# Attention steps over seven groups instead of six, the heads' norms in pieces of a quarter slab, and the output heads normed in two halves

## The chip, the cores and the metric

The kernel runs on one core of a Trainium2 chip. The metric is the device time of one launch in microseconds; the median of three runs stands for a kernel. TensorE (PE, with PEld for its weight loads), VectorE (DVE), ScalarE (ACT) and GpSimd (POOL) each run their own program in order and meet on semaphores; SyncE (SP) issues the DMAs.

## The reference, cut to what matters

Two transformer blocks are computed on 512 rows of 1024 columns, in float32. The first has a retention, a differential attention and a merge of both; the second a dilated-window attention and a latent attention. The change lies in the first block's differential attention, and in the inverse root that all RMS norms of the kernel share.

```python
def rms_norm(x, g):
    xf = x.astype(jnp.float32)
    xf = xf * lax.rsqrt(jnp.mean(xf * xf, axis=-1, keepdims=True) + EPS)
    return xf * g.astype(jnp.float32)
...
        qd = rms_norm(q_d.reshape(B, S, DIFF_HEADS, 2, DIFF_DK), diff_q_norm_g[l])
        kd = rms_norm(k_d.reshape(B, S, DIFF_HEADS, 2, DIFF_DK), diff_k_norm_g[l])
        o_d = diff_attention(qd, kd, v_d.reshape(B, S, DIFF_HEADS, DIFF_DV), lam)
        o_d = rms_norm(o_d, diff_sub_norm_g[l].reshape(DIFF_HEADS, DIFF_DV)) * (1.0 - lam_init)
        o_d = (o_d.reshape(B, S, DIFF_V) * jax.nn.silu(gate_d.astype(jnp.float32))).astype(x.dtype)
        y_d = jnp.einsum('bse,ed->bsd', o_d, diff_w_o[l])
```

`diff_attention` is a causal softmax attention with 8 heads; each head takes the difference of two softmaxes. Queries and keys are 64 wide (two of each per head), values 128 wide.

## The kernel before

**Groups, slabs, quarters.** All weight products are cut into 36 groups of up to 512 output columns (`GROUPS`). A group has 8 slabs in most cases, one for each 128 rows of the weight. A slab is four quarters, one for each block `t` of 128 rows of the input. A quarter is one product in three matmuls (`mm3`, lines 1548 to 1550), since each float32 operand is split into a high and a low part. For each slab SP brings the weights into `raw` (two slabs a transfer), ACT makes `w_hi` (line 481), POOL makes `w_lo` by subtraction (line 809), both three slabs ahead, and PE sums eight slabs in the banks `Z[0..3]`. At a group's end ACT or DVE takes the banks out.

**Which groups.** Groups 10, 11, 12 and 13 give queries, keys, values and gate of the heads 0 to 3 of the differential attention; 14, 15, 16 and 17 give the same of the heads 4 to 7. Groups 18 and 19 give the merge gate, 20 and 21 multiply the attention's output by `diff_w_o`, 22 and 23 by `w_out`. From group 24 on it is the second block; its attention lies between groups 33 and 34 (`attention`), without weight products beside it.

**The attention as filler.** The differential attention goes head by head in 32 tiles (8 heads by 4 row blocks), as a chain over engines: scores (PE, line 1680), bias and row extreme (DVE, line 1280), exponent (ACT, line 650), scaling (POOL, line 915), combination (DVE, line 1299), transposes (PE, line 1706), split (ACT 645, DVE 1286), output product (PE). Each engine has the chain as a generator of 86 steps, and `diff_due(v)` says how many steps are to be issued by quarter `v` of the attention's groups. In the kernel before these are groups 14 to 19 (`G_DIFF0 = 14`), 192 quarters: 36 steps by quarter 83, 22 more by 129, the last 28 by 163. An engine's program holds the same step at the same quarter as the others', and PE does its quarter's product first. So a step waits for a step before it of another engine, and has as cover the quarters between both. The first queries and keys are transposed at slab 5 of group 13.

**Norms of queries and keys.** The heads of groups 10 and 11 are normed before the attention begins; those of 14 and 15 within it, in slabs 1 to 5 of the group after. In `diff_slot` POOL squares one row block a slab (line 821, behind `lo`), DVE begins the slab with the sums of these squares (`head_sums`, line 1060), and at slab 5 it does `head_scale` in one piece: the inverse root (`rsqrt`, a seed and four Newton passes of three instructions; `link` makes each wait for the one before) and four scalings of 512 columns (line 1072). The transposes of head 4 wait for them (`head_normed`).

**Norm of the output.** A head's output in `A[3]` is squared by ACT (line 661) and multiplied by the gate into `o_sb` (DVE, line 1292, `o_out`). After all eight, at slab 4 of group 19, `scale_heads(diff=True)` makes the 32 inverse roots and scales `o_sb` in four pieces of 1024 columns (line 1156, `o_normed`). The transposes of `o_sb` for group 20 (`turn_when_ready`, line 1558) begin at slab 4 of group 19 and wait for all of it.

**Other users of `rsqrt`.** The norms of the rows (`row_rms`, in groups 0 and 24, ahead of DVE's part of the fifth transposed input block), the retention's heads, the latent vectors, and queries and keys of the second block.

## Time and profile before

| | us |
|---|---|
| median of the three runs | 1064.23 |
| lowest, highest | 1055.76, 1064.32 |
| profiled execution | 1065.86 |
| its span, first to last instruction | 1064.1 |
| PE busy, share of the span | 993.1, 93% |
| DVE, ACT, POOL busy | 449.7, 446.0, 498.1 |
| mean granted TensorE clock | 0.953 |

The profiled execution lies 1.6 us above the median of the runs. The engines' busy times overlap. PE's record holds every matmul; as matmuls are pipelined, a busy PE is not a PE at its peak, but an idle PE is lost time wherever it sets the end. A time in brackets behind a row is idle time of that engine just before it, with what ended it.

### The profile page before, as it was taken

Reading aid. Unit: us, or ns where it says so; the run is one execution under the profiler, and the core shown is the slowest. Engines: PE = TensorE matmul, PEld = TensorE weight load, DVE = VectorE, ACT = ScalarE, POOL = GpSimd, SP = SyncE. Lnnn points to the kernel's source line nnn. Section 1 sums busy time; section 2 is a strip of 40 time slices with the busy share of each in tenths; the row PEclk is TensorE's granted clock in tenths of the full one; section 3 lists DMA queues with packets and bytes.
Section 4 is the critical chain, followed back from the end, with each engine's and each line's share of the span. In section 5 each row is a group of like instructions: output and inputs, shape, how many; then the busy total and the mean of one; then the engine's idle time right before and its main releaser. Section 6 shows DMA issues by size and latency. Waiting matters only on the chain.

```text
span 1064.1 us, 14047 instructions
## 1 busy us (share of the span) xinstructions
PE 993.1 (93%) x5116; PEld 809.0 (76%) x5116; DVE 449.7 (42%) x1084; ACT 446.0 (42%) x992; POOL 498.1 (47%) x476
## 2 busy tenths in 40 slices
PE   6999989999999999797999899999999979999998
PEld 5777788876888877576777687788878756778877
DVE  3300478133204333545455523326552466458811
ACT  4333552334233345354565233236335315458821
POOL 2443534434457365354454334433754554545542
PEclk9999999999999999898999999999999985569999
DMA  6332211323333231111221241222422320110023
GB/s 203 97 83 77 80 40 41 99 59 99 99 89 105 84 93 50 47 51 40 60 61 40 65 174 60 99 79 76 118 75 85 88 80 20 30 31 2 2 64 115
DMA packets 41171, 78.76 MB, mean 74 GB/s; under 512 B 3296, under 2 KB 5088, under 8 KB 41104
## 3 DMA queue, kind: packets, MB, share of 16 engines
q1 hardware_dynamic: 41104, 77.87, 24.5%
q8 instruction: 41, 0.67, 0.3%
q14 instruction: 26, 0.21, 0.1%
HBM read 75.74 MB, written 2.12 MB: 73 GB/s over the span
## 4 chain that ended last, share of the span: by engine, by line
PE 69%; DVE 12%; issue 6%; ACT 6%; POOL 5%; DMA 1%; SPq 1%; ACTq 0%; DVEq 0%; POOLq 0%
PE Z L1548 20%; PE Z L1550 19%; PE Z L1549 19%; POOL w_lo L809 3%; PE A L1548 2%; PE A L1680 1%; PE A L1770 1%; PE A L1550 1%; PE A L1549 1%; PE A L1558 1%; ACT prob L697 1%; DVE rs_b L1028 1%; DVE rstd L1029 1%; DMA raw<-in_w_in 1%; POOL prob L821 1%
## 5 line engine op out<-in xcount | busy, mean ns | idle before, releaser
L809 POOL TENSOR_TENSOR w_lo<-raw,w_hi 128x512 fp32r<-128x512 f32 (+2 forms) x262 | 340.1, 1306 | 435.5 <-ACT w_hi L481 435.2
L1548 PE MATMUL Z<-w_hi,hT_hi 128*128 128x512 f32 (+1 forms) x832 | 336.8, 405 | 14.1 <-DVE hT_lo L1044 4.6
L1550 PE MATMUL Z<-w_hi,hT_lo 128*128 128x512 f32 (+1 forms) x832 | 325.9, 392 | 0.0
L1549 PE MATMUL Z<-w_lo,hT_hi 128*128 128x512 f32 (+1 forms) x832 | 325.6, 391 | 0.0
L481 ACT CAST w_hi<-raw 128x512 fp32r<-128x512 f32 (+2 forms) x262 | 157.5, 615 | 281.4 <-PE Z L1550 267.5
L1548 PEld LDWEIGHTS Z<-w_hi,hT_hi 128*128 128x128 f32 x832 | 157.9, 190 | 55.3 <-POOL w_lo L809 6.9
L1550 PEld LDWEIGHTS Z<-w_hi,hT_lo 128*128 128x128 f32 x832 | 157.6, 189 | 33.0
L1549 PEld LDWEIGHTS Z<-w_lo,hT_hi 128*128 128x128 f32 x832 | 158.1, 190 | 27.7
L1548 PE MATMUL Z<-w_hi,oT_hi 128*128 128x512 f32 x128 | 51.6, 403 | 3.3 <-DVE tmp L1101 2.2
L945 POOL TENSOR_SCALAR prob<-prob,rinv 128x128 f32<-128x128 f32 (+1 forms) x64 | 34.0, 532 | 36.9 <-DVE rinv L1363 35.6
L1550 PE MATMUL Z<-w_hi,oT_lo 128*128 128x512 f32 x128 | 50.1, 391 | 0.0
L1549 PE MATMUL Z<-w_lo,oT_hi 128*128 128x512 f32 x128 | 49.9, 390 | 0.0
L1060 DVE TENSOR_REDUCE stat<-bias 128x8 f32<-128x512 f32 (+2 forms) x32 | 18.4, 583 | 63.2 <-POOL bias L821 63.2
L650 ACT ACTIVATE x_sb<-x_sb,nmax 128x128 f32<-128x128 f32 (+3 forms) x64 | 35.5, 557 | 20.5 <-DVE nmax L1280 20.5
L1370 DVE TENSOR_TENSOR pT_lo<-A,pT_hi 128x128 fp32r<-128x128 f32 (+1 forms) x64 | 31.0, 484 | 27.5 <-ACT pT_hi L694 26.7
L694 ACT CAST pT_hi<-A 128x128 fp32r<-128x128 f32 (+1 forms) x64 | 26.8, 419 | 34.8 <-PE A L1770 34.6
L697 ACT ACTIVATE prob<-prob,nmax 128x128 f32<-128x128 f32 (+1 forms) x64 | 36.1, 564 | 11.9 <-DVE nmax L1347 11.9
L1121 DVE TENSOR_TENSOR x_sb<-x_sb,Z 128x512 f32<-128x512 f32 x16 | 10.9, 688 | 64.6 <-PE Z L1550 64.6
L1770 PE MATMUL A<-ident,prob 128*128 128x128 f32 x160 | 36.8, 338 | 0.7 <-POOL prob L945 0.7
L1280 DVE CUSTOM_DVE_ANT_0 x_sb<-A,bias 128x128 f32<-128x128 f32 (+3 forms) x64 | 28.7, 486 | 18.1 <-PE A L1680 18.0
L495 ACT ACTIVATE z_sb<-Z,rms 128x512 f32<-128x512 f32 (+1 forms) x40 | 26.5, 680 | 19.6 <-PE Z L1550 19.6
L1044 DVE SCALAR_TENSOR_TENSOR oT_lo<-A,cols,oT_hi 128x512 fp32r<-128x512 f32 x16 | 12.0, 751 | 48.3 <-ACT oT_hi L529 48.3
(286 smaller groups left out, 1716.2 us busy)
## 6 DMA issues: line engine op xcount, KB each, us to landing
raw<-in_w_in SPq DMA_DIRECT2D x92, 512.0 KB, 3.8
raw<-in_w_out SPq DMA_DIRECT2D x16, 512.0 KB, 3.6
raw<-in_ret_w_o SPq DMA_DIRECT2D x8, 512.0 KB, 3.5
raw<-in_diff_w_o SPq DMA_DIRECT2D x8, 512.0 KB, 3.5
x_sb<-in_x SPq DMA_DIRECT2D x8, 256.0 KB, 6.2
x_sb<-in_x SPq DMA_DIRECT2D x4, 512.0 KB, 5.7
bias<-bias_dram SPq DMA_DIRECT2D x8, 256.0 KB, 3.1
out<-x_sb SPq DMA_DIRECT2D x8, 256.0 KB, 3.2
```

Of the source, the lines that this page charges most:

```text
L481: act.copy(w_hi[:, s % SPLIT_SLOTS, 0:width], raw[:, c % RAW_SLOTS, s - CHUNK_START[c], 0:width]).then_inc(hi_ready, 1)
L650: act.activation(p, p, ACT.Exp, bias=nmax[:, j, n:n + 1], scale=-1.0, accum_out=rsum[:, n, j:j + 1]).then_inc(s_exp, 1)
L694: act.copy(pT_hi[:, m % 2, 0:wm], turn_bank(ph, m)[:, 0:wm]).then_inc(p_hi, 1)
L697: act.activation(prob_at(ph, 0, n, w), prob_at(ph, 0, n, w), ACT.Exp, bias=nmax[:, 0, n % 32:n % 32 + 1], scale=-1.0, accum_out=rsum[:, n ...
L809: pool.tensor_tensor(w_lo[:, s % SPLIT_SLOTS, 0:width], raw[:, c % RAW_SLOTS, s - CHUNK_START[c], 0:width], w_hi[:, s % SPLIT_SLOTS, 0:wid ...
L945: pool.tensor_scalar(p0, p0, rinv[:, m % 32, 0:1], 0.5, ALU.mult, ALU.mult).then_inc(s_scaled, 1)
L1280: dve.tensor_tensor_reduce(prob_at(DIFF, j, n, w), A[j][:, 0:w], bias[:, h % 2, S - w:S], -1.0, TOP, ALU.add, ALU.min, nmax[:, j, n:n + 1] ...
L1370: dve.tensor_tensor(pT_lo[:, m % 2, 0:wm], turn_bank(ph, m)[:, 0:wm], pT_hi[:, m % 2, 0:wm], ALU.subtract).then_inc(p_lo, 1)
L1548: pe.matmul(out, l_hi, r_hi, start=first, stop=False)
L1549: pe.matmul(out, l_hi, r_lo, start=False, stop=False)
L1550: return pe.matmul(out, l_lo, r_hi, start=False, stop=last)
L1770: last = pe.transpose(turn_bank(ph, m)[:, kk], prob_at(ph, 0, m, S)[:, kk], ident[:, :])
```

## The change

- The groups of the attention are 13 to 19 instead of 14 to 19: 224 quarters. The steps are due from quarter 10 on, and the last at quarter 208 of these (quarter 176 counted as before). The first transposes of queries and keys move from slab 5 to slab 1 of group 13.
- POOL squares two row blocks in each of the slabs 0 and 1 of groups 15 and 16; DVE takes the sums at four places two quarters apart.
- `head_scale` is a generator of eight pieces, one in each quarter of slabs 3 and 4: three times a part of the inverse root, then part and scalings.
- `scale_heads(diff=True)` becomes `diff_heads_normed(half)`, once for heads 0 to 3 in slabs 5 and 6 of group 17, once for heads 4 to 7 in the same slabs of group 19. The first four transposes of `o_sb` wait for the first half alone, the next four for the second. The one into `A[3]` waits for the last head's output to be taken.
- `rsqrt` has three Newton passes instead of four, for all its users.

```diff
-G_QD, G_DIFF, G_DIFF0, G_DIFF1 = 10, 13, 14, 19
+G_QD, G_DIFF, G_DIFF0, G_DIFF1 = 10, 13, 13, 19
...
+DIFF_FIRST, DIFF_SECOND, DIFF_THIRD, DIFF_LAST = 10, 116, 160, 208
...
 def diff_due(v):
-    if v < 84:
-        return 36 * (v + 1) // 84
-    if v < 130:
-        return 36 + 22 * (v - 83) // 46
-    return min(86, 58 + 28 * (v - 129) // 34)
+    if v < DIFF_FIRST:
+        return 0
+    if v < DIFF_SECOND:
+        return 36 * (v - DIFF_FIRST + 1) // (DIFF_SECOND - DIFF_FIRST)
+    if v < DIFF_THIRD:
+        return 36 + 22 * (v - DIFF_SECOND + 1) // (DIFF_THIRD - DIFF_SECOND)
+    return min(86, 58 + 28 * (v - DIFF_THIRD + 1) // (DIFF_LAST - DIFF_THIRD))
...
+def normed_in(g):
+    return in_diff(g) and g - 1 in HEAD_NORM and g - 1 > G_DIFF
...
-                if g - 1 in HEAD_NORM and 1 <= k <= TT:
-                    c0, t = HEAD_NORM[g - 1], k - 1
-                    pool.wait_ge(z_by_act, act_evacs[g - 1] + t + 1)
-                    square(z_sb[:, t, c0:c0 + 512], 512, diff=True)
-                for _ in range(diff_due(v + 3) - diff_due(v - 1)):
-                    next(steps)
+                if g == G_DIFF0 and k == 1:
+                    diff_bias(0)
+                    diff_values(0)
+                for half in range(2):
+                    if normed_in(g) and k < 2:
+                        c0, t = HEAD_NORM[g - 1], 2 * k + half
+                        pool.wait_ge(z_by_act, act_evacs[g - 1] + t + 1)
+                        square(z_sb[:, t, c0:c0 + 512], 512, diff=True)
+                    for _ in range(diff_due(v + 2 * half + 1) - diff_due(v + 2 * half - 1)):
+                        next(steps)
...
-            def rsqrt(n, parts=range(5)):
+            def rsqrt(n, parts=range(4)):
...
-                rsqrt(32)
+                for part in range(4):
+                    rsqrt(32, (part,))
+                    if part < 3:
+                        yield
                 for t in range(TT):
+                    yield
                     zz = z_sb[:, t, c0:c0 + 512].rearrange("p (h e) -> p h e", h=8)
...
+            def diff_heads_normed(half):
+                n = H // 2 * (half + 1)
+                dve.wait_ge(o_squared, TT * n)
+                dve.wait_ge(o_out, n)
...
+                for t in range(TT):
+                    yield
+                    o = o_sb[:, t, 512 * half:512 * half + 512].rearrange("p (h e) -> p h e", h=H // 2)
+                    r = rstd[:, 4 * t:4 * t + 4].unsqueeze(2).broadcast_to([P, H // 2, DV])
+                    dve.tensor_tensor(o, o, r, ALU.mult).then_inc(o_normed, 1)
...
-                if g - 1 in HEAD_NORM and 1 <= k <= TT:
-                    head_sums(k - 1, squares_d)
-                if g - 1 in HEAD_NORM and k == TT + 1:
-                    head_scale(HEAD_NORM[g - 1])
                 for t in range(TT):
+                    if normed_in(g) and 2 <= TT * k + t <= 8 and t % 2 == 0:
+                        head_sums(2 * k + t // 2 - 1, squares_d)
                     for _ in range(diff_due(v + t) - diff_due(v + t - 1)):
                         next(steps)
+                    if normed_in(g) and k in (3, 4):
+                        next(norms[g])
+                    if g == G_DIFF0 + 4 and k in (5, 6):
+                        next(norms["first"])
+                    if g == G_DIFF1 and k in (5, 6):
+                        next(norms["second"])
...
-                        pe.wait_ge(o_normed, 8)
+                        pe.wait_ge(o_normed, 4 * (half + 2))
...
+                if g == G_DIFF_OUT and k == 3:
+                    pe.wait_ge(o_out, H)
...
-                    if k == START_SLAB and g == G_DIFF:
+                    if k == 1 and g == G_DIFF0:
```

## Rows read from the trace of the kernel before

**Rows 1.** The page: engines' busy time over the span, and granted clock in 40 slices.

```profile
PE 993.1 (93%) x5116; PEld 809.0 (76%) x5116; DVE 449.7 (42%) x1084; ACT 446.0 (42%) x992; POOL 498.1 (47%) x476
...
PEclk9999999999999999898999999999999985569999
```

**Rows 2.** Windows at the group borders 13 to 19: length, each engine's busy time, PEclk.

```profile
356.30:380.20 23.90, 23.28 (x106) 18.71 (x105) 2.57 (x4) 8.77 (x16) 11.95 (x10) 1.00 0.22 65
...
411.10:456.60 45.50, 38.01 (x196) 29.63 (x196) 20.91 (x63) 19.61 (x53) 20.32 (x20) 0.92 0.17 47
456.60:501.50 44.90, 36.88 (x195) 28.09 (x194) 23.23 (x70) 20.37 (x62) 20.49 (x21) 0.92 0.17 48
...
583.30:614.30 31.00, 26.92 (x126) 22.13 (x125) 15.48 (x25) 11.06 (x25) 11.49 (x8) 0.94 0.21 68
sum 258.00, PE 236.00 PEld 184.58 DVE 116.23 ACT 125.47 POOL 116.77; mean PE 33.71 PEld 26.37 DVE 16.60 ACT 17.92 POOL 16.68
```

**Rows 3.** A window over group 11, a group without attention beside it.

```profile
312.80:334.50 21.70, 21.70 (x97) 17.98 (x96) 10.63 (x23) 7.43 (x13) 14.20 (x12) 1.00 0.34 97
```

**Rows 4.** Waits of PE, 356.3 to 614.3: us in total, times, longest.

```profile
PE A L1663 <- DVE z_sb L1072: 5.6, 1, 5.6
PE A L1663 <- DVE pT_lo L1286: 5.1, 3, 3.3
PE A L1680 <- DVE nmax L1280: 4.4, 2, 2.9
PE A L1558 <- DVE o_sb L1156: 4.1, 1, 4.1
PE A L1548 <- DVE o_sb L1292: 2.2, 4, 0.9
PE Z L1548 <- POOL w_lo L809: 0.5, 1, 0.5
```

**Rows 5.** Timelines of POOL, DVE and PE in slab 3 of group 15.

```profile
427.09 1.04 POOL L821 TENSOR_TENSOR prob<-z_sb 128x512 f32<-128x512 f32 x1
...
428.16 0.69 DVE L1060 TENSOR_REDUCE stat<-prob 128x8 f32<-128x512 f32 x1 [2.69 <-POOL prob L821]
...
430.28 0.33 PE L1680 MATMUL A<-kT_hi,qT_hi 64*128 64x128 f32 x2 [2.94 <-DVE nmax L1280]
```

**Rows 6.** Timelines of DVE and POOL: `head_scale` in groups 15 and 16.

```profile
438.64 1.29 POOL L809 TENSOR_TENSOR w_lo<-raw,w_hi 128x512 fp32r<-128x512 f32 x1 [1.43 <-ACT w_hi L481]
...
438.78 1.19 DVE L1028 SCALAR_TENSOR_TENSOR rs_b<-rs_b,rs_a 128x32 f32<-128x32 f32 x1
440.01 0.19 DVE L1029 SCALAR_TENSOR_TENSOR rstd<-rs_b,rstd 128x32 f32<-128x32 f32 x1
440.24 0.19 DVE L1027 TENSOR_TENSOR rs_b<-rstd 128x32 f32<-128x32 f32 x1
...
482.36 0.18 DVE L1068 TENSOR_SCALAR rs_a<-stat 128x32 f32<-128x32 f32 x1
...
486.69 2.50 DVE L1072 TENSOR_TENSOR z_sb<-z_sb,rstd 128x512 f32<-128x512 f32 x4
```

**Rows 7.** Timeline of DVE in group 19: inverse roots and scalings of the output.

```profile
587.43 0.18 DVE L1147 TENSOR_SCALAR rs_a<-stat 128x32 f32<-128x32 f32 x1
...
592.97 6.80 DVE L1156 TENSOR_TENSOR o_sb<-o_sb,rstd 128x1024 f32<-128x1024 f32 x4
```

**Rows 8.** Windows over the four stretches of lower clock in groups 15, 16 and 19, summed.

```profile
sum 17.10, PE 14.97 PEld 12.04 DVE 4.89 ACT 5.82 POOL 4.92; mean PE 3.74 PEld 3.01 DVE 1.22 ACT 1.45 POOL 1.23
```

**Rows 9.** Timeline of DVE in group 12: the last scalings ahead of the attention.

```profile
351.83 3.60 DVE L1072 TENSOR_TENSOR z_sb<-z_sb,rstd 128x512 f32<-128x512 f32 x4
```

**Rows 10.** Timelines of PE and DVE: waits outside groups 13 to 19.

```profile
29.17 0.50 PE L1548 MATMUL Z<-w_hi,hT_hi 128*128 128x512 f32 x1 [2.25 <-DVE hT_lo L1044]
...
724.53 0.16 DVE L1029 SCALAR_TENSOR_TENSOR rstd<-rs_b,rstd 128x4 f32<-128x4 f32 x1
...
856.49 0.79 PE L1548 MATMUL Z<-hT_hi,w_hi 128*128 128x512 f32 x1 [2.93 <-POOL w_lo L809]
```

**Rows 11.** Windows of the second attention, line 1347 alone: length, DVE busy, PEclk.

```profile
885.30:929.90 44.60, 7.89 (x33) 0.50 0.09 26
967.20:1006.80 39.60, 11.73 (x49) 1.00 0.01 2
```

More of the change, by code:

```diff
@@ L713, in diff_slot @@
                 hi(s + 3)
+                if g == G_DIFF0 and k == 1:
+                    diff_queries(0)
+                    diff_keys(0)
+                    diff_values(0)
                 if g + 1 in EARLY and k >= 4:
@@ L956, in diff_slot @@
                 lo(SLAB0[g] + k + 3)
-                if g - 1 in HEAD_NORM and 1 <= k <= TT:
-                    c0, t = HEAD_NORM[g - 1], k - 1
-                    pool.wait_ge(z_by_act, act_evacs[g - 1] + t + 1)
-                    square(z_sb[:, t, c0:c0 + 512], 512, diff=True)
-                for _ in range(diff_due(v + 3) - diff_due(v - 1)):
-                    next(steps)
+                if g == G_DIFF0 and k == 1:
+                    diff_bias(0)
+                    diff_values(0)
+                for half in range(2):
[5 more added lines that the diff above has]
+                        next(steps)
             steps = diff()
@@ L984, in _ @@
                         retention(k)
-                    if k == START_SLAB + 1 and g == G_DIFF:
-                        diff_bias(0)
-                        diff_values(0)
                     if k == START_SLAB + 1 and g == G_ATT2:
@@ L1037, in query_norms @@
                 rsqrt(64, (part,))
-                if part == 4:
+                if part == 3:
                     dve.engine_nop().then_inc(latent, 1)
@@ L1078, in head_norm @@
                     head_sums(t, bias)
-                head_scale(c0)
+                for _ in head_scale(c0):
+                    pass
             def take(g, t):
@@ L1137, in take_gates, with scale_heads @@
                                                  ALU.mult).then_inc(th_used, 1)
-            def scale_heads(diff=False):
-                if diff:
-                    dve.wait_ge(o_squared, TT * H)
-                    dve.wait_ge(o_out, H)
-                else:
-                    dve.wait_ge(sq_used, count["sq"])
-                sums = stat[:, 32:64] if diff else stat[:, 0:32]
-                link(dve.tensor_scalar(rs_a[:, 0:32], sums, 1.0 / DV, EPS, ALU.mult, ALU.add))
+            def diff_heads_normed(half):
+                n = H // 2 * (half + 1)
+                dve.wait_ge(o_squared, TT * n)
+                dve.wait_ge(o_out, n)
+                sums = stat[:, 32:64].rearrange("p (t h) -> p t h", t=TT)[:, :, n - H // 2:n]
+                link(dve.tensor_scalar(rs_a[:, 0:16].rearrange("p (t h) -> p t h", t=TT), sums, 1.0 / DV, EPS,
+                                       ALU.mult, ALU.add))
+                for part in range(4):
+                    rsqrt(16, (part,))
+                    if part < 3:
+                        yield
+                r4 = rstd[:, 0:16].rearrange("p (t h) -> p t h", t=TT)
+                link(dve.tensor_tensor(r4, r4, rms[:, 0, 0, :].unsqueeze(2).broadcast_to([P, TT, H // 2]), ALU.mult))
+                for t in range(TT):
+                    yield
+                    o = o_sb[:, t, 512 * half:512 * half + 512].rearrange("p (h e) -> p h e", h=H // 2)
+                    r = rstd[:, 4 * t:4 * t + 4].unsqueeze(2).broadcast_to([P, H // 2, DV])
+                    dve.tensor_tensor(o, o, r, ALU.mult).then_inc(o_normed, 1)
+                yield
+            def scale_heads():
+                dve.wait_ge(sq_used, count["sq"])
+                link(dve.tensor_scalar(rs_a[:, 0:32], stat[:, 0:32], 1.0 / DV, EPS, ALU.mult, ALU.add))
                 rsqrt(32)
-                if diff:
-                    r4 = rstd[:, 0:32].rearrange("p (t h) -> p t h", t=TT)
-                    link(dve.tensor_tensor(r4, r4, rms[:, 0, 0, :].unsqueeze(2).broadcast_to([P, TT, H]), ALU.mult))
                 for t in range(TT):
@@ L1305, in diff, with diff_slot @@
                     yield
-            def diff_slot(g, k, steps):
+            def diff_slot(g, k, steps, norms):
                 v = TT * (KD * (g - G_DIFF0) + k)
-                if g - 1 in HEAD_NORM and 1 <= k <= TT:
-                    head_sums(k - 1, squares_d)
-                if g - 1 in HEAD_NORM and k == TT + 1:
-                    head_scale(HEAD_NORM[g - 1])
+                if g == G_DIFF0 and k == 1:
+                    diff_queries(0)
+                    diff_keys(0)
                 for t in range(TT):
+                    if normed_in(g) and 2 <= TT * k + t <= 8 and t % 2 == 0:
+                        head_sums(2 * k + t // 2 - 1, squares_d)
                     for _ in range(diff_due(v + t) - diff_due(v + t - 1)):
                         next(steps)
+                    if normed_in(g) and k in (3, 4):
[4 more added lines that the diff above has]
+                        next(norms["second"])
                     if k == KD - 1:
@@ L1474, in _ @@
             steps = diff()
+            norms = {G_DIFF0 + 2: head_scale(HEAD_NORM[G_DIFF0 + 1]), G_DIFF0 + 3: head_scale(HEAD_NORM[G_DIFF0 + 2]),
+                     "first": diff_heads_normed(0), "second": diff_heads_normed(1)}
             for g in range(NG):
@@ L1477, in _ @@
                     for k in range(KD):
-                        diff_slot(g, k, steps)
+                        diff_slot(g, k, steps, norms)
                     continue
@@ L1821, in project @@
                         pe.wait_ge(pair_lo, k + 1)
-                    if k == START_SLAB and g == G_DIFF:
+                    if k == 1 and g == G_DIFF0:
                         pe.wait_ge(head_normed, 8)
```

14 lines of the change are left out of this document (4 added, 10 removed).

## The prediction

> **What bounds the kernel now.** I read the page first. PE is busy for 93% of the span, and no other engine for half of it [rows 1]. So PE's own program sets the end, and a change can give back only three things: PE's idle time, a lower granted clock under its work, and PE's work itself. The change takes no matmul away. The question is how much of the first two lies where the change works.
>
> Windows at the group borders come next. Groups 13 to 19 take 258.0 us with 236.0 us of busy PE, so PE idles for 22.0 us there [rows 2]. A group without attention beside it takes 21.7 us with PE never idle [rows 3]. The idle time is not spread: groups 15 and 16 hold 7.5 and 8.0 us of it, group 19 holds 4.1 us, and in just these three the mean clock is below 1 [rows 2].
>
> The waits of PE in this stretch name the causes, 21.9 us in all [rows 4]. The reader should see that five of the six rows end on DVE, though DVE is busy for only 116.2 us of the 258.0 us [rows 2]. DVE is not short of time; it is late at certain places. The timelines show them. In slab 3 of group 15 POOL's square ends at 428.13, DVE's sum starts at 428.16 after 2.69 us of idleness, the row extremes of the attention queue behind it, and PE gets its scores going at 430.28, 2.94 us late [rows 5]. `head_scale` in group 16 runs from 482.36 to 489.19 [rows 6], and the transposes of head 4 wait 5.6 us for it [rows 4]. The norm of the output runs from 587.43 to 599.77 [rows 7], and the transposes of `o_sb` wait 4.1 us.
>
> Last the clock. Four stretches of together 17.10 us were granted half speed (1.2 instead of 2.4 GHz) in groups 15, 16 and 19. They hold 14.97 us of PE's work [rows 8], and each follows a wait of 2.9 us or more. Work at half speed takes twice the time, so they cost 14.97 / 2 = 7.5 us.
>
> **The change part by part.** What could be won in groups 13 to 19 is 21.9 + 7.5 = 29.4 us, and the stretch would take 228.6 us.
>
> Sums of squares. Before, every slab from 1 to 4 begins on DVE with a wait for POOL, whose square stands behind `w_lo` of the same slab. Waits of this kind are both of line 1280 (4.4 us) and two of the three on line 1286 (5.1 less the longest 3.3, 1.8 us), together 6.2 us [rows 4]. After, the squares are done in slabs 0 and 1, two each. The first sum stands at quarter 2 of slab 0. With slabs of about 4.5 us beside the attention, quarter 2 comes 2.2 us after the slab's start. The square is ready after `w_hi`, `w_lo` (1.3 us) and its own 1.04 us [rows 5, 6], and ACT still has a bank of the last group to empty: some 4 us. DVE is then late by 2 us there and by less at each next sum. The cover is what counts: in the first phase a step is due every 106/36 = 2.9 quarters of 1.1 us, 3.2 us, where it was 84/36 = 2.3 quarters, 2.6 us. And with the new order no step with row extremes of group 16 lies right behind the first sum. I take 0.5 us as what stays. From both sides: nothing, or the whole 6.2 us and as much again if POOL, with two squares a slab, makes both DVE and its own scaling late.
>
> Scaling of queries and keys. One piece of 6.8 us (482.36 to 489.19) [rows 6] becomes eight. An instruction of the inverse root comes 0.23 us after the last (440.01 to 440.24), and there are 12 of them instead of 15 with the first one: 2.8 us. A scaling takes 2.50 / 4 = 0.63 us. So a piece takes about 0.7 us and lies in a quarter of 1.1 us, in which the attention needs DVE for 0.4 us on average. It has the cover of 2.9 quarters, so it is priced at nothing. The last piece is at quarter 3 of slab 4, and the transposes of head 4's keys are at quarter 1 of slab 5. Gone: 5.6 us and the longest of line 1286 (3.3 us). Without that cover, each of the pieces would cost PE its length.
>
> A row speaks against pieces beside POOL: while `w_lo` ran at 438.64, an instruction of 0.19 us took 1.19 us [rows 6]. The Trainium skill (GPSIMD Engine Reference, section Specifications) says that the SBUF interfaces are shared with VectorE and that instructions with two SBUF inputs contend. By that rule, if each of 32 pieces were held once, DVE would spend 32 us more. The row has one instruction held in each POOL operation, in the kernel before too, and the sum goes by it.
>
> Norm of the output. The first half is done two groups early. The second half has its roots and scalings (2.8 + 4 × 0.63, about 5.4 us) in slabs 5 and 6 of group 19, while PE needs it only after slab 0 of group 20, two to three slabs of 3 us later. Gone: 4.1 us. What is late next is the last head's own output, which only the transpose into `A[3]` at slab 7 needs, over three slabs after the last step: nothing.
>
> Spread of the steps. The last 28 steps are due over 48 quarters instead of 34. The waits for line 1292 (2.2 us) are of outputs close behind one another; I leave 0.5 us. The 0.5 us of `w_lo` in group 13 stays and moves with the first transposes. The 86 steps cost PE the same work wherever they stand. The start at slab 1 of group 13 waits for scalings that end at 351.83 + 3.60 = 355.4 [rows 9], and PE reaches that slab 2.7 us after 356.3: nothing. If it were late, it would be by tenths. SP's loads of `x` behind the last step are held by the waits on `p_t` and `s_comb`; these move by 13 quarters, and the transfers are for group 22: nothing.
>
> With no wait near 3 us left, the four stretches of half speed go: 7.5 us. The Trainium skill (TensorE: Matmul & The Clock Gate, section Terms) gives the penalty as the throttled time times one less the ratio, here 17.10 / 2 = 8.6 us. The rows give 7.5 us, since PE was idle in a part of them; the difference is 1.1 us.
>
> In the stretch: 29.4, less 0.5 (sums), 0.5 (line 1292), 0.5 (`w_lo`), and 0.5 for pieces that come late once: 27.4 us.
>
> Three Newton passes. In `row_rms` three instructions less, 0.2 us apart (0.16 us busy) [rows 10], stand in front of what PE waits for in group 0 (2.25 us) and in the like place of group 24: 2 × 0.6 = 1.2 us. The 2.93 us wait for `w_lo` in group 33 [rows 10] has a square of POOL before it that waits for DVE's roots: 3 × 0.23 = 0.7 us. Elsewhere the roots lie beside work of PE. From nothing to 3 us, the upper if one of the shorter waits no longer brings a slow stretch.
>
> Sum: 27.4 + 1.9 = 29.3 us. The profiled execution of 1065.86 (span 1064.1 and 1.8 around it) becomes 1036.6. It stands 1.6 above the median of the runs, 1064.23; the forecast of the median is 1064.2 − 29.3 = 1035 us.
>
> **The rivals.**
>
> *The sums still stall PE.* For it: POOL gets 3.4 us of `w_lo` and squares into a slab of 4.5 us, and its scalings wait for DVE, which waits for its squares. Against it: the first steps of group 16 with row extremes come a slab later. The 6.2 us less 0.5 and one slow stretch (1.7 us) stay: 1035 + 7.4 = 1042 us; with twice the waits 1050 us.
>
> *The pieces stand in PE's way.* Four series of 2.8 + 2.5 = 5.3 us, all on the path, are 21 us: 1056 us. It decides once a step's cover is under a piece of 0.7 us plus its step. Against it: the dense end of the attention (0.82 steps a quarter) had idle PE for 0.9 us at most [rows 4].
>
> *The second attention runs at half speed for less time.* Line 1347 leaves two records a tile, eight a head. At clock 0.50 four heads took 44.6 us (33 records), at full clock six took 39.6 us (49 records) [rows 11]: 11.2 us a head against 6.6 us. So the clock there is worth far more than all waits. The three runs of one kernel lie 8.6 us apart, which I read as this. The shift could put it into the shorter case: 1035 − 8.6 = 1026 us. The Trainium skill (the same page, Part 1) says that the gate runs free of the kernel's start and that results vary by run; by that rule the shift favours no side, which is why this rival is small.
>
> *The other sign: it runs at half speed to its end.* Eight heads more at 4.6 us each are 37 us: 1072 us. From 29.3 / 4.6 = 6.4 heads more on, the gain is eaten. For it: the stretch begins after a wait of the gates ahead of it, which the change leaves. Against it: the runs shown lie within 8.6 us, less than two heads' worth.
>
> **How the numbers follow.** Chances: the forecast 0.55, sums still stall 0.20, shorter half speed 0.13, pieces in the way 0.07, longer half speed 0.05. The forecast's own range, from its open ends (nothing to 3 us outside, 0 to 4 us inside), is 1030 to 1041 us. The range of 8 in 10 takes in the second and third case with their spread, 1024 to 1050 us, and leaves out the last two. 1% is 10.6 us, about what a measurement can tell from no change; faster by more means below 1053.6. The first three cases lie below, 0.88; the fourth is within, with a part of the last: 0.09; slower keeps 0.03.
>
> **What would show it.** Groups 13 to 19 should take 230 to 232 us instead of 258.0. In PE's waits there, line 1072 and the output's scaling should be gone, and lines 1280 and 1286 together be under 1 us. The clock should be 1.00 in each group's window. DVE's scalings should stand singly between rows of the attention. The transposes of `o_sb` in group 19 should have no wait. It is wrong if new waits of over 1 us stand on POOL's squares or in slabs 3 and 4, or if the low slices of PEclk at the second attention (8, 5, 5, 6) [rows 1] become more or fewer.

## The result and the profile after

| | before | after |
|---|---|---|
| median, us | 1064.28 (4 runs, 1055.76 to 1065.07) | 1025.74 (4 runs, 1020.73 to 1034.31) |
| profiled execution and its span | 1065.86, 1064.1 | 1022.06, 1020.2 |
| mean granted TensorE clock | 0.953 | 0.979 |

The ratio is 0.966, with a 95% interval of 0.958 to 0.975. The ratios in this document and their intervals leave out runs that lay over 1.5% above the fastest of the same kernel; medians and ranges hold all runs. The forecast was 1035 us, range 1024 to 1050. The median moved by 38.5 us where 29.3 were forecast.

The spans of the two profiled executions differ by 43.9 us. Read at the group borders, they come from these places. Each is a difference of two windows or of two starts of a group.

| stretch | before | after | difference |
|---|---|---|---|
| start to group 13 | 356.3 | 352.2 | −4.1 |
| groups 13 to 19, the attention of the change | 258.0 | 233.5 | −24.5 |
| groups 20 to 32 | 228.7 | 227.4 | −1.3 |
| group 33, up to the second attention's first row extreme | 37.3 | 35.4 | −1.9 |
| second attention, to group 34 | 136.8 | 123.3 | −13.5 |
| groups 34 and 35 | 47.0 | 48.5 | +1.5 |

The page of the changed kernel first: the row of busy times and the granted clock in 40 slices, as in [rows 1].

```profile
PE 969.3 (95%) x5116; PEld 791.5 (78%) x5116; DVE 447.3 (44%) x1062; ACT 444.3 (44%) x992; POOL 501.2 (49%) x476
...
PEclk9999999999999999999999999999999997959999
```

PE has the same 5116 matmuls and 23.8 us less busy time, since less of its work was done at half speed. The slices below 9 in the middle are gone, and at the second attention there are fewer.

The windows over groups 13 to 19 of the changed kernel (columns as in [rows 2]), and PE's waits in them (as in [rows 4]):

```profile
352.20:378.90 26.70, 26.44 (x133) 20.65 (x131) 6.65 (x22) 13.44 (x31) 14.34 (x13) 1.00 0.27 83
...
411.00:442.20 31.20, 31.20 (x172) 24.66 (x170) 21.67 (x55) 16.74 (x44) 19.68 (x19) 1.00 0.22 68
442.20:478.10 35.90, 33.87 (x194) 26.29 (x192) 23.89 (x62) 19.18 (x55) 19.69 (x19) 1.00 0.19 60
...
556.70:585.70 29.00, 28.60 (x152) 23.59 (x151) 14.64 (x33) 13.20 (x31) 12.65 (x10) 1.00 0.22 73
sum 233.50, PE 228.85 PEld 179.31 DVE 122.01 ACT 123.82 POOL 116.95; mean PE 32.69 PEld 25.62 DVE 17.43 ACT 17.69 POOL 16.71
```

```profile
PE A L1699 <- DVE z_sb L1088: 2.0, 1, 2.0
PE A L1699 <- DVE pT_lo L1316: 1.0, 1, 1.0
PE A L1584 <- DVE o_sb L1324: 0.8, 2, 0.4
PE A L1716 <- DVE nmax L1310: 0.4, 1, 0.4
PE Z L1584 <- POOL w_lo L819: 0.3, 1, 0.3
PE Z L1584 <- DVE o_sb L1109: 0.2, 1, 0.2
```

Groups 15 and 16 went from 45.5 and 44.9 us [rows 2] to 31.2 and 35.9. The clock is 1.00 in every group in this profile. The waits fell from 21.9 us [rows 4] to 4.7. PE's busy time, 228.85 us, is what the prediction had as the stretch without any wait or slow clock (228.6 us). One wait of 2.0 us is left in group 16, again on the scaling of the keys.

The second attention, 13.5 us of the gain, holds none of the parts of the change that the forecast priced. Of the change it has only the shorter inverse roots of its queries. Windows over it and over its two stretches of half speed, in the changed kernel:

```profile
848.50:971.80 123.30, 116.29 (x916) 95.70 (x915) 91.19 (x307) 82.63 (x236) 71.40 (x105) 0.87 0.07 18
847.40:861.10 13.70, 13.42 (x50) 10.23 (x50) 10.59 (x41) 8.18 (x22) 6.93 (x10) 0.50 0.09 20
895.20:915.70 20.50, 20.50 (x105) 15.86 (x104) 10.08 (x34) 9.22 (x25) 6.99 (x12) 0.50 0.02 8
```

The same in the kernel before:

```profile
880.30:1017.10 136.80, 131.78 (x914) 107.73 (x915) 93.01 (x310) 82.74 (x236) 71.44 (x105) 0.74 0.06 17
...
879.80:937.80 58.00, 57.21 (x266) 43.74 (x266) 32.61 (x114) 26.86 (x77) 31.23 (x44) 0.50 0.08 24
944.60:958.30 13.70, 13.70 (x70) 10.60 (x68) 7.10 (x23) 6.22 (x18) 3.18 (x7) 0.50 0.02 8
```

The matmuls are the same in number; half speed lasted 71.7 us before and 34.2 us after.

### The profile page after: what moved, and what is told of

Read it like the earlier page. It is cut to its first block, busy times and chain, and to the rows that moved or that the text cites. A ratio compares the mean times of both kernels' runs of the same rounds, so it can differ in the third digit from the quotient of the medians.

```text
span 1020.2 us, 14034 instructions
## 1 busy us (share of the span) xinstructions
PE 969.3 (95%) x5116; PEld 791.5 (78%) x5116; DVE 447.3 (44%) x1062; ACT 444.3 (44%) x992; POOL 501.2 (49%) x476
## 4 chain that ended last, share of the span: by engine, by line
PE 73%; DVE 10%; ACT 6%; issue 5%; POOL 5%; DMA 1%; SPq 1%; ACTq 0%; DVEq 0%; POOLq 0%
PE Z L1584 22%; PE Z L1586 21%; PE Z L1585 21%; POOL w_lo L819 2%; PE A L1584 2%; PE A L1716 2%; PE A L1586 1%; PE A L1585 1%; PE A L1594 1%; ACT prob L707 1%; PE A L1806 1%; DMA raw<-in_w_in 1%; PE A L1742 1%; ACT w_hi L491 1%; DVE m_sb L1134 1%
## 5 line engine op out<-in xcount | busy, mean ns | idle before, releaser
L1585 PEld LDWEIGHTS Z<-w_lo,hT_hi 128*128 128x128 f32 x832 | 156.6, 188 | 27.4
L1806 PE MATMUL A<-ident,prob 128*128 128x128 f32 x160 | 32.8, 307 | 2.8 <-POOL prob L955 2.7
L655 ACT CAST pT_hi<-A 128x128 fp32r<-128x128 f32 (+3 forms) x32 | 13.7, 427 | 47.6 <-PE A L1742 47.5
```

Source lines behind the costliest of these rows:

```text
L1585: pe.matmul(out, l_hi, r_lo, start=False, stop=False)
L1806: last = pe.transpose(turn_bank(ph, m)[:, kk], prob_at(ph, 0, m, S)[:, kk], ident[:, :])
```

## The experiments

The stretch of groups 13 to 19 is named "the stretch" here. Its length in a profile is the sharp measure, since kernels that share its code agree in it by a few tenths of a microsecond plus what the clock does in it. What the clock does is not little. Two of the experiments below, "square early" and "latent steps spread", leave the stretch as the changed kernel has it, and their profiles show the same waits, to 0.1 us. Yet in both a stretch of 3.4 us at half speed came after the 2.0 us wait in group 16. Their windows over groups 13 to 19, in this order:

```profile
353.40:588.40 235.00, 230.33 (x1265) 180.11 (x1265) 121.97 (x334) 123.91 (x338) 117.16 (x113) 0.99 0.22 64
357.90:592.90 235.00, 230.35 (x1266) 180.14 (x1265) 121.96 (x334) 124.00 (x338) 116.94 (x113) 0.99 0.22 64
```

So the same code took 233.5, 235.0 and 235.0 us, and 1.5 us of a difference can be the clock alone. The median of the whole program is blurred by the clock at two places. One lies about 165 us from the start: in six of the fourteen profiles, with edits of the kernel before and of the changed one among them, 10.2 or 13.7 us at half speed lie there, and group 13 begins at 357.6 to 359.2 us instead of 352.1 to 356.3. The other is the second attention. Together they show in the unchanged kernel: the kernel before had medians of 1064.37 (7 runs), 1064.74 (13), 1054.47 (17) and 1054.15 us (11) on the four occasions on which it was run beside the experiments (each on another chip), and single runs from 1046.45 to 1072.49 us.

### Three passes alone

```diff
-            def rsqrt(n, parts=range(5)):
+            def rsqrt(n, parts=range(4)):
```

> The kernel before with three Newton passes instead of four, nothing else. Groups 13 to 19 should keep their 258 us less 1.4 (two times three instructions of 0.23 us in the pieces that stall PE). Theory 'phase' (the 15.5 us that group 33 with the second attention lost between before and after, 174.2 to 158.7, are a matter of where the clock's state falls, not of the edit): about 1064 - 2 - 1.4 = 1061 us, and half speed in the second attention for about as long as before, some 70 us. Rival 'roots' (the shorter query norms at the start of the second attention keep the clock up): 1064 - 3 - 15 = 1046 us, with half speed there for under 40 us.

Measured 1046.9 us (1039.3 to 1049.2) beside 1064.4, ratio 0.986 (0.978 to 0.995). The stretch took 255.9 us, 2.1 less than before where 1.4 were expected: 0.8 us of idle time and one stretch of half speed fewer. The second attention took 121.5 us. By the numbers on record this spoke for the rival. The next run tells otherwise.

### Four passes in the changed kernel

```diff
-            def rsqrt(n, parts=range(4)):
+            def rsqrt(n, parts=range(5)):
```

> The changed kernel with four Newton passes as before; the fifth part of each root stands with the fourth piece. Theory 'phase': 1026 + 2 = 1028 us, group 33 stays near 159 us; pieces a little longer, the wait of 2.0 us for line 1088 in group 16 grows by under 1 us. Rival 'roots': group 33 goes back to 174 us, total 1043 us.

Measured 1031.7 us (1029.4 to 1034.1). The second attention took 121.3 us with four passes. So the roots don't set its clock, and the rival falls. The stretch took 236.3 us, 2.8 more than the changed kernel's profile: 1.3 us of idle time and one stretch of 3.4 us at half speed. That stretch came with three passes too, in the two profiles shown above, and against their 235.0 us the fourth pass costs 1.3 us.

### The output's norm at once

```diff
-                    if g == G_DIFF0 + 4 and k in (5, 6):
-                        next(norms["first"])
-                    if g == G_DIFF1 and k in (5, 6):
-                        next(norms["second"])
...
                 if g + 1 in EARLY and k >= 4:
+                    if k == 4:
+                        for _ in norms["first"]:
+                            pass
+                        for _ in norms["second"]:
+                            pass
```

> The changed kernel, but the output heads' two halves are both normed at slab 4 of group 19, one behind the other. Theory 'the halves save their wait': the transposes of o_sb wait for the first half, about 5 us with 2.8 us of roots and 2.5 us of scalings, and one stretch of half speed (1.7 us) returns: +5 to +7 us on groups 13 to 19, 1032 us. Rival 'the wait is hidden anyway since the steps end where the transposes begin': +1 us or less.

The stretch took 241.5 us, 8.0 more than with the halves; the forecast was +5 to +7. The median does not show it (1025.5 us). PE's waits in the stretch of this kernel:

```profile
PE A L1595 <- DVE o_sb L1175: 5.9, 1, 5.9
PE A L1700 <- DVE z_sb L1088: 2.0, 1, 2.0
```

The wait for the output's scaling is back, and longer than the 4.1 us of before, because the attention now ends right in front of the transposes. Idle time in the stretch rose by 4.4 us and PE's busy time by 3.5 us, since 10.2 us at half speed came back. Of these, 3.4 us lie in group 16, which the edit leaves alone, behind the same 2.0 us wait as in the profiles of 235.0 us. Against those the halves are worth 6.5 us, within the forecast. That they save a wait is shown.

### Queries' and keys' norms at once

```diff
-                for half in range(2):
-                    if normed_in(g) and k < 2:
-                        c0, t = HEAD_NORM[g - 1], 2 * k + half
+                if normed_in(g) and 1 <= k <= TT:
+                    c0, t = HEAD_NORM[g - 1], k - 1
...
+                if normed_in(g) and 1 <= k <= TT:
+                    head_sums(k - 1, squares_d)
+                if normed_in(g) and k == TT + 1:
+                    for _ in norms[g]:
+                        pass
...
-                    if normed_in(g) and 2 <= TT * k + t <= 8 and t % 2 == 0:
-                        head_sums(2 * k + t // 2 - 1, squares_d)
...
-                    if normed_in(g) and k in (3, 4):
-                        next(norms[g])
```

> The changed kernel, but queries' and keys' norms in groups 15 and 16 as before: one square a slab in slabs 1 to 4, the sum at the slab's start, roots and scalings in one piece at slab 5. Theory 'pieces and early squares save the waits': the waits of 6.2 us (sums) and 8.9 us (scalings), and two or three stretches of half speed (5.8 us) return in part, since a step now has 2.9 quarters of cover instead of 2.3: +9 to +19 us, 1035 to 1045 us. Rival 'the wider spread of the steps is what saves them': +4 us or less.

The stretch took 243.2 us, 9.7 more than in the changed kernel's profile and 8.2 more than the 235.0 us of the other two: about the low end of the first theory (9), and over the rival's 4. The median was 1033.0 us. The waits of this kernel:

```profile
PE A L1700 <- DVE z_sb L1088: 5.6, 1, 5.6
PE A L1700 <- DVE pT_lo L1316: 3.9, 3, 2.6
PE A L1585 <- DVE o_sb L1324: 0.8, 2, 0.4
PE A L1717 <- DVE nmax L1310: 0.4, 1, 0.4
```

The scaling costs nearly what it did before: 5.6 and 2.6 us. But the sums, which cost 6.2 us before [rows 4], are in at most 3.9 − 2.6 + 0.4 = 1.7 us here, with the squares placed as before, and the same lines cost 1.0 + 0.4 = 1.4 us in the changed kernel. So with the wider spread the early squares were not needed.

### Seven groups alone

The changed kernel with the last three edits at once: four passes, both norms at once.

> The changed kernel with norms of queries, keys and output at once and four passes: what is left of the change is the table over seven groups and the early start. Theory 'spread alone does little': groups 13 to 19 at 250 to 258 us. Rival 'spread does most': 240 us or less. The waits for POOL's squares (lines of the extremes, 6.2 us before) should fall by over half by either, since the cover goes from 2.6 to 3.2 us.

The stretch took 252.0 us, 6.0 less than before: the first theory by its range. The median was 1045.4 us beside 1064.7, ratio 0.986 (0.980 to 0.992). PE's waits in it:

```profile
PE A L1596 <- DVE o_sb L1175: 6.5, 1, 6.5
PE A L1701 <- DVE z_sb L1088: 6.2, 1, 6.2
PE A L1701 <- DVE pT_lo L1316: 3.5, 2, 3.3
PE A L1586 <- DVE o_sb L1324: 0.8, 2, 0.4
PE Z L1586 <- POOL w_lo L819: 0.3, 1, 0.3
PE A L1718 <- DVE nmax L1310: 0.2, 1, 0.2
```

Against [rows 4] the extremes' 4.4 us are 0.2, and line 1286's 5.1 us are 3.5, of which 3.3 are the scaling's. The sums cost 0.4 us instead of 6.2. In exchange the wait for the output grew from 4.1 to 6.5 us.

### Six groups with the new norms

```diff
-G_QD, G_DIFF, G_DIFF0, G_DIFF1 = 10, 13, 13, 19
+G_QD, G_DIFF, G_DIFF0, G_DIFF1 = 10, 13, 14, 19
...
+    if v < 84:
+        return 36 * (v + 1) // 84
+    if v < 130:
+        return 36 + 22 * (v - 83) // 46
+    return min(86, 58 + 28 * (v - 129) // 34)
```

> The changed kernel with the step table and the start of the kernel before (groups 14 to 19, first transposes at slab 5 of group 13), with the pieces, early squares, halves and three passes kept. Theory 'pieces': the long waits stay gone; groups 13 to 19 take about 236 to 240 us, the pieces being 0.5 to 3 us late more often with 2.3 quarters of cover. Rival 'spread': half of the 24.5 us gained in these groups goes, 246 us.

The stretch took 236.0 us: the first theory, at the good end. The median was 1026.7 us beside 1064.7, ratio 0.968 (0.962 to 0.974). The norms and the passes give 22.0 us of the 24.5 without any new spread; the spread adds 2.5 us on top of them, both at full clock. By itself it had given 6.0 us: the parts overlap. The waits are 7.2 us here and 4.7 us in the changed kernel:

```profile
PE A L1582 <- DVE o_sb L1322: 2.2, 4, 0.9
PE A L1697 <- DVE pT_lo L1314: 1.6, 2, 0.8
PE A L1697 <- DVE z_sb L1086: 1.2, 1, 1.2
PE A L1714 <- DVE nmax L1308: 1.1, 2, 0.7
```

So a cover of 2.3 quarters is enough for the pieces. The sums, 6.2 us before, are in at most 1.6 + 1.1 = 2.7 us here, so the early squares take most of their waits away without the spread as well. The waits for line 1322, 2.2 us as in [rows 4], are what the table over seven groups brings down (to 0.8 us), as forecast.

### Pieces ahead of the steps

```diff
+                    if normed_in(g) and k in (3, 4):
+                        next(norms[g])
...
                     for _ in range(diff_due(v + t) - diff_due(v + t - 1)):
                         next(steps)
-                    if normed_in(g) and k in (3, 4):
-                        next(norms[g])
```

> The changed kernel with each piece of the norms ahead of the attention's steps of its quarter, not behind them. Theory 'the fourth scaling stands behind a step': in the changed kernel it started at 465.93, behind 1.6 us of a step's work, and the transposes of head 4's keys waited 2.0 us; the wait goes to under 0.6 us and groups 13 to 19 take 231.5 to 232.5 us instead of 233.5. Rival 'the series is late as a whole, held by GpSimd operations (three instructions of 0.2 us took 1.2 us or more)': the wait stays over 1.5 us, 233.5 us or more since steps are later too.

The stretch took 232.0 us, 1.5 less than in the changed kernel at the same full clock, and the 2.0 us wait for the scaling is gone; the waits for line 1316 grew from 1.0 to 1.7 us. The median was 1023.5 us beside 1054.5, ratio 0.970 (0.964 to 0.976). DVE in group 16 of the changed kernel, and POOL beside it, show why it was there:

```profile
456.56 1.28 POOL L819 TENSOR_TENSOR w_lo<-raw,w_hi 128x512 fp32r<-128x512 f32 x1 [1.50 <-ACT w_hi L491]
458.98 1.29 POOL L819 TENSOR_TENSOR w_lo<-raw,w_hi 128x512 fp32r<-128x512 f32 x1 [1.14 <-ACT w_hi L491]
460.23 1.28 POOL L913 TENSOR_TENSOR v_lo<-z_sb,v_hi 128x512 fp32r<-128x512 f32 x1
```

```profile
456.60 1.28 DVE L1038 TENSOR_TENSOR rs_b<-rstd 128x32 f32<-128x32 f32 x1
...
459.04 1.27 DVE L1038 TENSOR_TENSOR rs_b<-rstd 128x32 f32<-128x32 f32 x1
460.35 1.21 DVE L1039 SCALAR_TENSOR_TENSOR rs_b<-rs_b,rs_a 128x32 f32<-128x32 f32 x1
461.60 0.19 DVE L1040 SCALAR_TENSOR_TENSOR rstd<-rs_b,rstd 128x32 f32<-128x32 f32 x1
...
464.85 0.55 DVE L1310 CUSTOM_DVE_ANT_0 x_sb<-A,bias 128x384 f32<-128x384 f32 x1
...
465.93 0.68 DVE L1088 TENSOR_TENSOR z_sb<-z_sb,rstd 128x512 f32<-128x512 f32 x1
```

Three POOL operations each held one instruction of the root: 1.28, 1.27 and 1.21 us instead of 0.19, 3.2 us in all. The series ran late, and its last scaling stood behind a step of the attention. The second part was needed for the wait: this experiment took it away, and the wait went, though three instructions of the root were still held (1.28, 0.62 and 1.21 us, 2.5 us in all). Whether the first part was needed too was not tested.

### The last square of the query norms early

```diff
                 for k in range(3, n):
+                    if g == G_QHEADS + 1 and k == KD - 2:
+                        query_square(k + 1)
                     lo(SLAB0[g] + k)
...
-                    if g == G_QHEADS + 1 and k < KD - 1:
+                    if g == G_QHEADS + 1 and k < KD - 2:
                         query_square(k + 1)
```

In the changed kernel:

> The changed kernel, with POOL's last square of the query norms put ahead of w_lo of slab 6 in group 33. VectorE then no longer waits 7.4 us for it and can take the gates' banks as they come. Theory 'the 4.1 us wait ahead of the second attention brings the half speed in': the wait falls to about 1.5 us, the clock stays up at the start, and with 4.6 us a head at stake the second attention gets 10 to 25 us shorter: 1000 to 1015 us. Rival 'the attention's own thin work brings it in': 2.6 us are won and the half speed stays: 1023 us.

In the kernel before:

> The kernel before with the same move of POOL's last square. Theory 'the wait brings it in': half speed in the second attention falls from 72 us to under 35, 1064 - 2.6 - 15 = 1046 us or lower. Rival 'thin work': 1061 us.

The wait ahead of the second attention fell from 4.1 to 2.1 us in both. Up to the attention's first row extreme the changed kernel needed 31.7 us instead of 35.4. But half speed came all the same: for 34.1 us from the attention's very start in the changed kernel (median 1026.0 us, no gain over 1025.7), for 10.2 and 17.1 us in the kernel before (1052.8 us from 1046.1 to 1055.2, beside 1064.7; ratio 0.991, 0.988 to 0.994). One outcome looked like the theory and the other like its rival, so neither stands: the length of the wait doesn't decide.

### A longer wait in the kernel before

```diff
                 if g == G_ATT2:
                     attention(start=True)
+                    for _ in range(8):
+                        link(dve.tensor_copy(rs_b[:, 0:32], rs_a[:, 0:32]))
```

> The kernel before with 1.8 us of small VectorE copies ahead of the gates' last banks, so that the wait ahead of the second attention is longer and the attention starts later. Theory 'alignment' (half speed there lasts long when the attention's start meets the point where the clock falls; any shift, earlier or later, takes the kernel before out of it): 1064 + 1.8 - 12 = 1054 us, about 30 us of half speed. Rival 'a longer wait is worse': 1066 us or more, 70 us of half speed or more. Third, 'chance': runs of both kinds as in the kernel before, median within 3 us of 1066.

Measured 1056.1 us (1049.2 to 1068.1), but the kernel before, run beside it, had 1054.5 us this time (1047.5 to 1071.6). The ratio is 1.002 (0.998 to 1.006), or +1.6 us, which is the added work. The wait was 5.8 us, and half speed lasted 13.7 us at the start. So a longer wait is not worse either. Of the two theories left, "alignment" and "chance" are not told apart by the median: 1056.1 us is 2 us off the first's 1054, but the unedited kernel had 1054.5 itself.

### Latent steps spread over more tiles

```diff
+                latent_at = [n for n in range(6, 27) if n not in (13, 20, 21)]
                 for n in range(N + 8):
                     h, i = divmod(n, 4)
-                    if 6 <= n < 3 * TT + 12:
-                        latent_queries(n - 6)
+                    if n in latent_at:
+                        latent_queries(latent_at.index(n))
```

> The changed kernel with POOL's 18 latent-query operations of the second attention spread over 21 tiles, leaving out three tiles in which POOL has another operation of 1.3 or 0.7 us. Theory 'the 1.35 us wait for POOL's scaling brings in the second stretch of half speed (20.5 us in the changed kernel, 17 us in six others)': wait under 0.5 us, the stretch gone or shorter, 1026 - 1 - 5 = 1020 us. Rival 'the attention's own thin work does it': the stretch stays, 1025 us.

PE's waits for POOL's scalings fell from 2.7 to 1.5 us, the longest from 1.4 to 0.8. The second stretch of half speed stayed, 13.7 us instead of 20.5. The attention took 119.2 us in the profile, the shortest of all, but the six runs were 1016.8, 1022.7, 1026.4, 1042.8, 1043.1 and 1043.1 us. That is inconclusive for the edit, and no trace shows what the three longer runs did. The wait of 1.4 us was not what brings this stretch in, since it fell to 0.8 and the stretch stayed; the theory had asked for under 0.5 us.

### Both moves together

The changed kernel with the pieces ahead of the steps and the last square early.

> The changed kernel with two moves: the norms' pieces ahead of the attention's steps of their quarter, and POOL's last square of the query norms ahead of w_lo of slab 6 in group 33. Outside the second attention both should add up: groups 13 to 19 at 232 us, and 31.7 us instead of 35.4 us from group 33's start to the second attention, 5 us less than the changed kernel in all. The second attention stays as alignment has it: 121 us with about 30 us of half speed where the clock falls more than 1 us off the attention's start, 129 us or more where it falls within 0.6 us of it. Median 1021 us, runs from 1014 to 1030 us. If the clock's stretches followed the wait ahead of the attention (2.1 us here instead of 4.1), no run should show more than 30 us there and all be under 1020 us.

Windows of this kernel over the stretch, over group 33 up to the second attention, over that attention, and over its first part at half speed:

```profile
352.40:584.60 232.20, 228.90 (x1265) 179.32 (x1264) 121.82 (x334) 123.83 (x338) 118.16 (x113) 1.00 0.22 65
811.80:843.80 32.00, 25.53 (x112) 19.20 (x110) 24.45 (x53) 11.87 (x21) 17.08 (x16) 1.00 0.22 67
843.80:974.10 130.30, 123.45 (x915) 101.15 (x915) 91.55 (x307) 82.45 (x236) 71.33 (x105) 0.80 0.06 17
843.80:877.90 34.10, 33.66 (x151) 25.72 (x152) 19.75 (x74) 15.80 (x47) 16.40 (x25) 0.50 0.09 24
```

Measured 1020.9 us (1019.8 to 1028.9) beside 1054.2, ratio 0.973 (0.968 to 0.978). The two moves add up: 232.2 us in the stretch and 31.7 us in group 33 (its window above starts 0.3 us early), 1.3 and 3.7 us less than the changed kernel. The profiled execution had the clock fall at the attention's very start and half speed for 34.1 us, as the alignment theory says. The median is 4.9 us under the changed kernel's 1025.7, as expected. Since the two were not timed beside one another and the second attention scatters by more than that, only the stages are shown to be faster, not the whole.

## Why the prediction was right, point by point

**What bounds the kernel: right.** PE's idle time and clock were the gain. 22.0 us of idle time in the stretch became 4.7 us, four stretches of half speed became none, and PE's busy time there is 228.85 us where the prediction's floor was 228.6. That none was left is partly luck. The prediction let all four go "with no wait near 3 us left", but a wait of 2.0 us stayed, and behind it one stretch came back in three of the four profiles that have that wait at 2.0 us. By the signs that the prediction named, the stretch took 233.5 us for 230 to 232, the scaling's wait was 2.0 us and not gone, and the two lines of extremes and splits had 1.4 us and not under 1. The low slices at the second attention became fewer, which it had named as a sign of being wrong, and that holds for the part of the gain outside its sum.

**The size in the stretch: 24.5 us of the 27.4.** In the other two profiles of this code it was 23.0 us. The missing 2.9 us are the 4.7 us of waits that stayed, where 2.0 us were allowed for. The term that was mis-sized is the price of the pieces: "priced at nothing", with 0.5 us for pieces that come late once, and 2.0 us measured. It put one instruction held by each POOL operation down as costless, because the kernel before had it too. Three held instructions (3.2 us) made the series late, and its last scaling, placed behind a step of the attention, reached PE 2.0 us late; with the pieces ahead of the steps that wait was gone. The Trainium skill (GPSIMD Engine Reference, section Specifications) says that GpSimd's SBUF interfaces are shared with VectorE, and that VectorE instructions with two SBUF inputs contend. The trace agrees, with about 1.0 to 1.1 us per POOL operation of 1.28 us. The 32 us that the prediction worked out from this rule for every piece did not come: DVE is busy for 122.0 us in the stretch against 116.2 us before.

**The cover: the mechanism was real, its role was misplaced.** The prediction let the pieces be free because a step has 2.9 quarters of cover instead of 2.3. With 2.3 quarters the stretch took only 2.5 us more (236.0 us), and the scaling's wait was 1.2 us instead of 2.0. For the sums the prediction credited the cover and the early squares together. Either is nearly enough: the cover alone took their waits from 6.2 to 0.4 us, the early squares alone to at most 2.7.

**The output's halves: right.** 4.1 us and a share of the half speed, 5.8 us in all, were forecast; undone, they cost 8.0 us, of which 1.5 are the clock in group 16 that the edit does not touch. The attention ends later in the table over seven groups, and the wait for the norm at once is longer there (5.9 us with three passes, 6.5 us with four) than before. So the new table needs the halves.

**Three passes: right, and a little more.** Outside the stretch 1.2 us were forecast for `row_rms` and 0.7 for group 33. Group 24 gave 1.3 us by itself (its wait is gone). Group 33 up to the attention gave 1.9 us, but the changed kernel with four passes needed 36.0 us there, so the passes are worth 0.6 of it; the rest goes with half speed, 6.8 us there in the kernel before and 3.4 us in the changed kernel with either number of passes. At the start the wait in group 0 fell from 2.25 us [rows 10] to 1.25 us, and no stretch of half speed followed; that and 1.75 us of an earlier arrival of `x`, which is not the change's, make the 4.1 us of the first row of the table.

**The second attention: a rival that came true beside the forecast.** "Half speed for less time" had 0.13 and 8.6 us. It gave 13.5 us between the profiles. As far as the runs show, this is luck and not the work of any part of the change: four passes or three, six groups or seven, the attention took 119 to 123 us in nine of fourteen profiles and 129 to 137 us in five, the kernel before and the last version (both moves) among the five. The kernel before also moved by 10 us between occasions. Against its median of 1054.3 us on the later two, the changed kernel's 1025.7 us would be 28.6 us less, which is the forecast's 29.3. Against 1064.3 it is 38.5. Both are measured, but the first is put together from different occasions. Chip and occasion changed together, so what moved the kernel before is open, and so is why the changed kernel's relatives did not move with it: 1026.0 and 1026.7 us beside 1064.7, 1023.5 beside 1054.5. A mere shift of the program may matter, since one small move in group 33 made the kernel before about 10 us faster (ratio 0.991), and only 2 us of that are in group 33. The part that the stages show for the change is 23.0 to 24.5 us in the stretch, 1.3 us in group 24, 0.6 to 1.9 us in group 33 and some 1 to 2 us at the start. The prediction also read the 8.6 us between three runs as the second attention alone; the half speed near 165 us is a second source of it, and moves group 13 by about 6 us.

## What to carry to other kernels

Where one engine sets the end and another is half idle, look at where the second is late, not at how busy it is: cutting its long series into pieces, with the shorter root, gave 22.0 of 24.5 us, and spreading the main work on top gave 2.5 (6.0 by itself). A piece of VectorE must be priced with the GpSimd operations that run beside it, and it belongs ahead of a step, not behind it, if its result has a due time. And when a stage without any edit moves by more than a per cent, time the stages by the profile and compare the kernel before on several occasions before giving the change the credit.

## What the runs showed of the hardware

**Half speed with a busy PE.** In the second attention the granted clock fell to 1.2 GHz at or near its start in all fourteen profiles, and stayed there for 10.2 to 58.0 us although PE was busy for nearly all of it: 57.21 of 58.00 us in the kernel before. Behind the first head, one wholly at half speed took 10.5 to 12.5 us, one wholly at full speed 6.2 to 8.2. The Trainium skill (TensorE: Matmul & The Clock Gate, Part 1) says that activity releases the throttle and that the gate runs free of the kernel's start. The second fits the runs, in which the fall lay from 2.4 us before to 1.4 us after the attention's first row extreme, but none of them tests it. The first is not what these rows look like, with 58.0 us at half speed under a PE that was busy by the profile.

**How long it lasted went with where it fell.** The start of the first stretch of half speed against the first row extreme of the attention, with the stretch's length:

| kernel | fell at, us | lasted, us |
|---|---|---|
| before | −0.5 | 58.0 |
| six groups, new norms | −0.5 | 30.7 |
| pieces ahead | −0.6 | 30.7 |
| changed, square early | 0.0 | 34.1 |
| both moves | 0.0 | 34.1 |
| changed | −1.1 | 13.7 |
| heads at once; output at once | −1.4; −1.3 | 13.7; 13.7 |
| latent steps spread | −1.4 | 13.7 |
| three passes | −1.7 | 13.7 |
| four passes; seven groups alone | −2.1; −2.2 | 13.7; 13.7 |
| longer wait | −2.4 | 13.7 |
| before, square early | +1.4 | 10.2 |

Five profiles with the fall within 0.6 us of the attention's start have 30.7 us or more, nine others have 13.7 us or less. This is a pattern in fourteen profiles and not a shown cause. The last of the five came after this was put down as an expectation. Why the kernel before had 58 us and not 31 to 34 is open, and so is which share of runs falls into which case: each run gives a time, but only one of each kernel has a trace. That the place of the fall is drawn anew in each run is likely from the spread of the runs, but was not shown on traces of one kernel.

**A small VectorE instruction beside a GpSimd operation.** An instruction of the inverse root, on 128x32 elements in most places, takes 0.16 to 0.23 us where no operation of GpSimd runs beside it. One that began over 0.03 us after one of GpSimd's operations of 1.28 us on 128x512 elements, while it ran, did not end before it. In all fourteen profiles, 329 of 329 such instructions ended 0.02 to 0.09 us behind the GpSimd operation. So the loss is what is left of that operation, up to 1.1 us, and one instruction pays it for each operation. It held for instructions with one input too, as in this pair of the kernel before, where the second of two GpSimd operations ended at 177.76:

```profile
175.22 2.54 POOL L809 TENSOR_TENSOR w_lo<-raw,w_hi 128x512 fp32r<-128x512 f32 x2
176.58 1.21 DVE L1024 TENSOR_SCALAR rs_b<-rs_a 128x32 int32<-128x32 int32 x1
```
